# Rounding half of the output projection's inputs inside the attention, and issuing one half block there, in the two attention layers

## The reference, cut to what matters

```
# odd: 16 heads of 128, over the keys that a top-k picks
logits = einsum('bqhd,bqkd->bqhk', qb, kg) * (128 ** -0.5)
p = softmax(where(valid, logits, -inf));  o = einsum('bqhk,bqkd->bqhd', p, vg)
x = x + gate * ((o * silu(g)) @ odd_w_out)        # (512 x 2048) @ (2048 x 1024)
# fox: 16 heads of 64, causal, with a decay of the keys
x = x + (o * silu(gate)) @ fox_w_out              # (512 x 1024) @ (1024 x 1024)
```

## Time and profile before

| | us |
|---|---|
| median of 3 runs (lowest, highest) | 1831.99 (1830.11, 1836.62) |
| the profiled execution, its own time | 1826.95 |
| its span | 1825.2 |
| TensorE matmul busy | 1728.3 (95%) |
| VectorE busy | 1267.1 (69%) |
| GpSimd busy | 817.8 (45%) |
| ScalarE busy | 807.8 (44%) |

### The profile page before, as it was taken

One profiled execution on the slowest core, in us unless ns is written; L12 is line 12 of the kernel. 1 busy time (PEld: TensorE's weight loads), 2 busy tenths in 40 slices (PEclk: granted clock), 3 DMA queues, 4 the chain that ended last, 5 costly groups with the idle time before them and its releaser, 6 DMA issues.

```text
span 1825.2 us, 32731 instructions
## 1 busy us (share of the span) xinstructions
PE 1728.3 (95%) x13216; PEld 1282.1 (70%) x13216; DVE 1267.1 (69%) x2285; ACT 807.8 (44%) x1500; POOL 817.8 (45%) x721
## 2 busy tenths in 40 slices
PE   5999999999999979999999999899999999999987
PEld 5677777777777657767776666587677787777756
DVE  7599999999998676269986665634687617155553
ACT  3435345345343262365434443434577534344443
POOL 3534344344342245457871111255455555544433
PEclk9999999999999989999999999999999999999999
DMA  7212212212213124212221001022222232333312
GB/s 294 93 48 94 90 52 94 83 59 94 84 59 128 37 68 135 94 57 81 81 81 47 30 29 46 16 101 81 93 83 77 70 106 79 126 122 127 110 50 92
DMA packets 51878, 154.73 MB, mean 85 GB/s; under 512 B 5889, under 2 KB 12033, under 8 KB 51601
## 3 DMA queue, kind: packets, MB, share of 16 engines
q1 hardware_dynamic: 51728, 152.65, 24.9%
HBM read 150.50 MB, written 2.13 MB: 84 GB/s over the span
## 4 chain that ended last, share of the span: by engine, by line
PE 62%; DVE 19%; ACT 5%; issue 5%; POOL 5%; DMA 1%; DVEq 0%; SPq 0%; POOLq 0%; ACTq 0%
PE bank L504 14%; PE bank L508 13%; PE bank L505 13%; PE bank L1249 6%; PE bank L2244 3%; PE bank L2232 3%; PE bank L2266 2%; POOL w_lo L486 2%; DVE lru_xc L2686 2%; DVE best L2353 2%; DVE ya L1554 2%; DVE score L2356 2%; DVE raw L728 1%; PE bank L2899 1%; DMA raw<-even_in 1%
## 5 line engine op out<-in xcount | busy, mean ns | idle before, releaser
L486 POOL TENSOR_TENSOR w_lo<-raw,w_hi 128x512 fp32r<-128x512 f32 (+2 forms) x434 | 570.7, 1333 | 767.7 <-ACT w_hi L468 767.4
L504 PE MATMUL bank<-h_hi,w_hi 128*128 128x512 f32 x1368 | 585.4, 428 | 26.6 <-ACT h_hi L948 8.6
L508 PE MATMUL bank<-h_lo,w_hi 128*128 128x512 f32 x1368 | 545.2, 399 | 9.1 <-DVE h_lo L922 5.4
L505 PE MATMUL bank<-h_hi,w_lo 128*128 128x512 f32 x1368 | 541.8, 396 | 0.0
L468 ACT ACTIVATE w_hi<-raw 128x512 fp32r<-128x512 f32 (+2 forms) x434 | 241.9, 599 | 254.8 <-PE bank L508 179.9
L504 PEld LDWEIGHTS bank<-h_hi,w_hi 128*128 128x128 f32 x1368 | 261.8, 191 | 116.6 <-issue 48.3
L508 PEld LDWEIGHTS bank<-h_lo,w_hi 128*128 128x128 f32 x1368 | 260.7, 191 | 78.7 <-DVE h_lo L922 10.1
L505 PEld LDWEIGHTS bank<-h_hi,w_lo 128*128 128x128 f32 x1368 | 262.3, 192 | 57.1 <-issue 11.1
L1554 DVE SCALAR_TENSOR_TENSOR ya<-padded,vecs,ya 128x512 f32<-128x512 f32 x240 | 217.0, 904 | 3.3
L2301 ACT ACTIVATE probs<-probs,small 128x512 f32<-128x512 f32 x64 | 46.3, 724 | 108.9 <-DVE small L2284 108.5
L2968 DVE CUSTOM_DVE_ANT_0 fox_probs<-bank,fox_keybias 128x128 f32<-128x128 f32 (+3 forms) x64 | 28.8, 488 | 84.8 <-PE bank L2899 84.5
(11 more groups left out here) (398 smaller groups left out, 2796.6 us busy)
## 6 DMA issues: line engine op xcount, KB each, us to landing
raw<-even_in SPq DMA_DIRECT2D x57, 512.0 KB, 3.7
raw<-odd_in SPq DMA_DIRECT2D x39, 512.0 KB, 3.4
raw<-ada SPq DMA_DIRECT2D x32, 512.0 KB, 4.4
raw<-fox_in SPq DMA_DIRECT2D x25, 512.0 KB, 3.5
raw<-lru_in SPq DMA_DIRECT2D x24, 512.0 KB, 3.5
ada_first<-ada SPq DMA_DIRECT2D x16, 512.0 KB, 13.6
raw<-even_out SPq DMA_DIRECT2D x16, 512.0 KB, 3.5
raw<-odd_out SPq DMA_DIRECT2D x16, 512.0 KB, 3.4
```

The source lines that it names most:

```text
L486: e.tensor_tensor(k.w_lo[s % NSPLIT][:, at], k.raw[n % NRAW][:, at], k.w_hi[s % NSPLIT][:, at].bitcast(F32), ALU.subtract).then_inc(*did(" ...
L504: e.matmul(out, hi[:, w], x[i][0], start=start and i == 0, stop=False, skip_group_check=True)
L505: e.matmul(out, lo[:, w], x[i][0], start=False, stop=False, skip_group_check=True)
L508: m = e.matmul(out, hi[:, w], x[i][1], start=False, stop=stop and i == kt - 1, skip_group_check=True)
```

## The change: what it does, and the diff

1. In both layers the first half of the inputs (tiles 0 to 7 in odd, 0 to 3 in fox) is split inside the attention, after the last gate block is projected. ScalarE's `own_high` gets labels behind that block: 59.4 to 62.9 in odd (items 60 to 63 are the last), 30.7 to 31.6 in fox. GpSimd's `own_low` follows its last weight split of the stage.
2. Who makes the low parts: in odd all 8 of the first half are now GpSimd's (before, VectorE made 5 of them). In fox tiles 1 and 2 stay VectorE's, with labels 31.2 and 31.5, and 0 and 3 GpSimd's.
3. TensorE: half block (0,0) is issued between the attention's last transposes and products (labels 64.6 to 66.4 in odd, 32.3 to 33.1 in fox). Half block (1,0) stands behind the last product, as before.
4. The second half's splits wait for the last value product and for the last steps of VectorE, ScalarE and GpSimd in the attention (`attention_left`), and no longer for TensorE's last projection.

```
 def own_rest(s, i):
-    return ("made" if i % 3 else "pooled", "own_lo", s, i)
+    return ("pooled" if i % 3 == 0 or s == "odd" and i < AH // 2 else "made", "own_lo", s, i)
+def attention_left(k, stage, last):
+    return [("multiplied", *last)] + [("end", stage, engine) for engine in ("vector", "scalar", "gpsimd")]
...
+def out_block(k, e, need, did, s, name, pairs, cb, part, times):
...
+    return project(k, e, need, did, (name, cb, part), k.out_bank[cb], pairs[a:a + half],
+                   lambda i: [("activated", "own_hi", s, a + i), own_rest(s, a + i)], times, part == 0, part == 1)
...
+def og_time(i):
+    return gate_times(AH - 1)[-1] + 0.3 + 0.5 * i
...
 # odd_tensor
+    def out_blocks():
+        for cb in range(2):
+            at = AH * TT + 0.5 + 4 * cb
+            yield from out_block(k, e, need, did, "odd", "odd_out", k.odd_out[0], cb, 0, [at + (i + 0.5) / 4 for i in range(DT)])
     merge(in_tiles(AH * TT, (0, front), (LAG, back), (LAG + 1, at_head_end(finish))),
-          chain(*(block(("g", g), [("made", "gate", g)], gate_times(g)) for g in range(3, AH))))
+          chain(*(block(("g", g), [("made", "gate", g)], gate_times(g)) for g in range(3, AH)), out_blocks()))
...
 # odd_scalar
+    def early():
+        for i in range(AH // 2):
+            yield og_time(i)
+            own_high(e, need, did, "odd", i, k.odd_out[0], og_source(k), [("made", "og", i), ("projected", ("g", AH - 1))])
...
 # odd_gpsimd
     for g in range(3, AH):
         ahead(("g", g))
+    for i in range(AH // 2):
+        own_low(e, need, did, "odd", i, k.odd_out[0], og_source(k), [])
...
+def fox_y_time(i):
+    return fox_end("fox_g", DT - 1) + 0.1 + 0.3 * i
...
 # fox_tensor
+    def out_blocks():
+        for cb in range(2):
+            at = FOX_TILES + 0.2 + 3 * cb
...
 # fox_vector
+    def early():
+        for i in range(DT // 2):
+            if own_rest("fox", i)[0] == "made":
+                yield fox_y_time(i) + 0.2
+                own_low(e, need, did, "fox", i, k.fox_out[0], fox_y_source(k), [])
...
 # fox_scalar
+            yield fox_y_time(i)
+            own_high(e, need, did, "fox", i, k.fox_out[0], fox_y_source(k),
+                     [("made", "fox_y", i), ("projected", ("fox_g", DT - 1))])
...
 # fox_gpsimd
+    for i in range(DT // 2):
+        if own_rest("fox", i)[0] == "pooled":
+            own_low(e, need, did, "fox", i, k.fox_out[0], fox_y_source(k), [])
```

More of the change, by code:

```diff
@@ L247, in begin @@
         self.stat_until = ()
+        self.out_bank = {}
         if rehearsal:
@@ L954, in own_low, with out_tensor, out_scalar @@
     e.tensor_tensor(pairs[i][1], src(i), pairs[i][0].bitcast(F32), ALU.subtract).then_inc(*did(*own_rest(s, i)))
[L957 to L973, removed]
+def out_block(k, e, need, did, s, name, pairs, cb, part, times):
+    half = len(pairs) // 2
+    if part == 0:
+        k.out_bank[cb] = k.acc.take(("made", "x", s, cb))
+        k.bank[name, cb] = k.out_bank[cb][0]
+    a = part * half
+    return project(k, e, need, did, (name, cb, part), k.out_bank[cb], pairs[a:a + half],
+                   lambda i: [("activated", "own_hi", s, a + i), own_rest(s, a + i)], times, part == 0, part == 1)
+def out_tensor(k, e, need, did, s, name, pairs, sq, nxt, last=(), both=False, done=0):
+    times = out_times(len(pairs) // 2)
+    merge(*last, chain(*(out_block(k, e, need, did, s, name, pairs, cb, part, times[cb, part])
+                         for cb, part in out_order()[done:])))
     square_tensor(k, e, need, did, nxt, both, sq)
-def out_scalar(k, e, need, did, s, name, pairs, src, src_ready, sq, nxt, stage, last=(), beside=(), gain=None, early=0):
+def out_scalar(k, e, need, did, s, name, pairs, src, src_ready, sq, nxt, stage, last=(), beside=(), gain=None, early=0, free=None):
     n = len(pairs)
     def split(i):
-        own_high(e, need, did, s, i, pairs, src, [*src_ready(i), *k.ended(stage)])
+        own_high(e, need, did, s, i, pairs, src, [*src_ready(i), *(free or k.ended(stage))])
     def blocks():
@@ L1007, in out_vector @@
 def out_vector(k, e, need, did, s, name, pairs, src, src_ready, sq, nxt, stage, x_ready, gate=None, gate_ready=None,
-               last=(), beside=(), both=False, early=0):
+               last=(), beside=(), both=False, early=0, free=None):
     n = len(pairs)
     def split(i):
-        own_low(e, need, did, s, i, pairs, src, k.ended(stage))
+        own_low(e, need, did, s, i, pairs, src, free or k.ended(stage))
     def squares(i):
@@ L1045, in out_vector, with out_gpsimd @@
     merge(*last, *beside, blocks())
-def out_gpsimd(k, e, need, did, s, name, pairs, src, src_ready, stage, last=(), early=0):
+def out_gpsimd(k, e, need, did, s, name, pairs, src, src_ready, stage, last=(), early=0, free=None):
     n = len(pairs)
     def split(i):
-        own_low(e, need, did, s, i, pairs, src, k.ended(stage))
+        own_low(e, need, did, s, i, pairs, src, free or k.ended(stage))
     def blocks():
         yield 0.0
-        for i in range(early, n - 1, 3):
-            split(i)
+        for i in range(early, n - 1):
+            if own_rest(s, i)[0] == "pooled":
+                split(i)
         for b, (cb, part) in enumerate(out_order()):
@@ L2115, in gate_times, with og_source @@
     return [at + (i + 0.5) / 1.75 for i in range(DT)]
+def og_time(i):
+    return gate_times(AH - 1)[-1] + 0.3 + 0.5 * i
+def og_source(k):
+    return lambda i: k.Q[:, i, :]
 def turning(k, n):
@@ L2248, in odd_tensor @@
     turned = lambda i: [turn_done("odd", i)]
+    def out_blocks():
+        for cb in range(2):
+            at = AH * TT + 0.5 + 4 * cb
+            yield from out_block(k, e, need, did, "odd", "odd_out", k.odd_out[0], cb, 0, [at + (i + 0.5) / 4 for i in range(DT)])
     merge(in_tiles(AH * TT, (0, front), (LAG, back), (LAG + 1, at_head_end(finish))),
-          chain(*(block(("g", g), [("made", "gate", g)], gate_times(g)) for g in range(3, AH))))
+          chain(*(block(("g", g), [("made", "gate", g)], gate_times(g)) for g in range(3, AH)), out_blocks()))
     k.end("tensor", "odd")
-    out_tensor(k, e, need, did, "odd", "odd_out", *k.odd_out, "lru", both=True)
+    out_tensor(k, e, need, did, "odd", "odd_out", *k.odd_out, "lru", both=True, done=2)
     k.end("tensor", "odd_out")
@@ L2414, in odd_vector @@
                k.odd_out[1], "lru", "odd", lambda i: [("made", "x", "even", i)],
-               lambda i: k.mods[1][:, 2 * DT + i:2 * DT + i + 1], ("made", "mod", 1, 3 * DT - 1), both=True,
+               lambda i: k.mods[1][:, 2 * DT + i:2 * DT + i + 1], ("made", "mod", 1, 3 * DT - 1), both=True, early=AH // 2,
+               free=attention_left(k, "odd", ("attended", AH - 1)),
                beside=[lru_rates_vector(k, e, need, did), gain_squares_vector(k, e, need, did)])
@@ L2493, in back @@
             e.activation(dst, src, ACT.Copy).then_inc(*did("activated", "turned_odd", i))
-    merge(in_tiles(AH * TT, (0, middle), (LAG, back)), chain(*(gate_in(g, gate_times(g)[-1] + 0.2) for g in range(3, AH))))
+    def early():
+        for i in range(AH // 2):
+            yield og_time(i)
+            own_high(e, need, did, "odd", i, k.odd_out[0], og_source(k), [("made", "og", i), ("projected", ("g", AH - 1))])
+    merge(in_tiles(AH * TT, (0, middle), (LAG, back)), chain(*(gate_in(g, gate_times(g)[-1] + 0.2) for g in range(3, AH))), early())
     k.end("scalar", "odd")
     out_scalar(k, e, need, did, "odd", "odd_out", k.odd_out[0], lambda i: k.Q[:, i, :], lambda i: [("made", "og", i)],
-               k.odd_out[1], "lru", "odd", gain=lambda i: k.vec("final_g", i),
+               k.odd_out[1], "lru", "odd", gain=lambda i: k.vec("final_g", i), early=AH // 2,
+               free=attention_left(k, "odd", ("attended", AH - 1)),
                beside=[lru_rates_scalar(k, e, need, did)])
@@ L2536, in odd_gpsimd @@
         ahead(("g", g))
+    for i in range(AH // 2):
+        own_low(e, need, did, "odd", i, k.odd_out[0], og_source(k), [])
     k.end("gpsimd", "odd")
-    out_gpsimd(k, e, need, did, "odd", "odd_out", k.odd_out[0], lambda i: k.Q[:, i, :], lambda i: [("made", "og", i)], "odd")
+    out_gpsimd(k, e, need, did, "odd", "odd_out", k.odd_out[0], lambda i: k.Q[:, i, :], lambda i: [("made", "og", i)], "odd", early=AH // 2,
+               free=attention_left(k, "odd", ("attended", AH - 1)))
     k.end("gpsimd", "odd_out")
@@ L2917, in finish @@
         k.work.give(bank, ("made", "fox_y", p))
-    merge(projections(2, None), in_tiles(FOX_TILES, (0, front), (FOX_LAG + 1, at_pair_end(finish)), (FOX_LAG, back)))
+    def out_blocks():
+        for cb in range(2):
+            at = FOX_TILES + 0.2 + 3 * cb
+            yield from out_block(k, e, need, did, "fox", "fox_out", k.fox_out[0], cb, 0,
+                                 [at + (i + 0.5) / 4 for i in range(DT // 2)])
+    merge(chain(projections(2, None), out_blocks()),
+          in_tiles(FOX_TILES, (0, front), (FOX_LAG + 1, at_pair_end(finish)), (FOX_LAG, back)))
```

(8 more changed lines are left out.)

14 lines of the change are left out of this document (9 added, 5 removed).

## The result

| us | before | after |
|---|---|---|
| median, first comparison (6 runs each) | 1833.65 | 1824.26 (1819.45 to 1828.05) |
| ratio, 95% interval | | 0.9946 (0.9925 to 0.9966) |
| profiled execution; span | 1826.95; 1825.2 | 1823.81; 1822.1 |
| TensorE, VectorE busy | 1728.3, 1267.1 | 1729.5, 1260.3 |

The changed kernel is faster by 0.54% (0.34 to 0.75%). The forecast was a gain of 4.0 us, to 1828.0, with a range from 1822.5 to 1832.5. The median lies in the range, but the gain between the medians, 9.4 us, is more than twice the forecast, while the two profiled spans differ by 3.1 us only. Most of what follows is about that gap.

What follows compares the result with a forecast made beforehand. TensorE was taken as the bound (matmuls for 95% of the span), so time is won only where it idles or runs slowly. Odd 3.7 plus fox 1.7 less clock 1.4 gave 4.0 us gained, 1828.0 us, range 1822.5 to 1832.5.

Steps and rivals of the forecast that it cites:

- rival A: Whole kernel: full gain, no new low clock stretch or weights sooner than added up; 5.4 to 8 us gained; chance 0.33.
- same: Whole kernel: outcome within 0.3% (5.5 us), about what a measurement can tell from no change; chance 0.58.
- ScalarE's roundings push head 14's product to 1160.8: Odd's attention end: 4.2 us of new roundings delay the copy this product needs, and so its start, by only 1.2 us.
- Eight tiles ahead of the last product, none waiting for GpSimd; last product at 1171.5: Odd, TensorE: half block (0,0)'s 5.6 us stand ahead, low parts ready in time; last product starts 5.6 us later than 1165.94.
- A new wait for `w_lo` ahead of (0,1), start at 1181.9: Odd: weights come last, TensorE waits 1.2 us, and (0,1) starts at 1181.9 in place of 1185.63, 3.7 us gained.
- the list behind (0,1): Odd, TensorE: everything behind (0,1)'s start is the same instructions, busy 5.60 of 5.60 us, and moves as one.
- Fox, 1.7 us: Fox's tail: division 2.1 us late, last product 2.5, yet (0,1) 1.4 us earlier and tile 7 in time; 1.7 us gained.
- The contention rule set aside: Odd, VectorE divisions beside GpSimd subtractions: the skill's full-block rule would lose 5.4 us; one 0.53 us division was read against it.
- The clock, "one new low stretch in the two places", -1.4 us: Odd's and fox's tails: new TensorE idle times of 3.1 and 2.4 us bring one 1.2 GHz stretch, costing 1.4 us.
- "A shift in one stage carries over" to the median: Whole kernel: the profiled execution's 4.0 us gain passes to the median, which stands 5.0 us above it, giving 1828.0 us.

Runs made afterwards that it cites:

- e4: Changed kernel with half block (0,1)'s weight split moved ahead of the second half's roundings (ScalarE) and low parts (GpSimd), both layers: 1821.93 us, 0.9935 of the kernel before.
- e6: Changed kernel with VectorE again making five of odd's first eight low parts, as before the change: 1832.90 us, ratio 0.9997 to the kernel before.
- e3: Changed kernel with early roundings kept in both layers, but half block (0,0) put back behind the attention: 1829.09 us, ratio 0.9981 to the kernel before.
- c1: The kernel before, unchanged, timed against itself: 1831.71 us against 1834.56, ratio 0.9980.

## Why the prediction was right or wrong

The median fell inside the range, but partly by luck: the working holds 4.0 us of gain, and it was the width of the range that took in 9.4. The outcome is rival A's (1824 to 1826.5), whose condition, no new low stretch in the two tails, held in odd always and in fox in three of four profiles; its sum of 5.4 us is still not 9.4. Of the three outcomes, "same" had 0.58 and the one that came, faster by more than 0.3%, had 0.36.

- **ScalarE's roundings push head 14's product to 1160.8:** right, 1160.54; the copy ended 1.0 us later, forecast 1.2.
- **Eight tiles ahead of the last product, none waiting for GpSimd; last product at 1171.5:** right, 1170.92. GpSimd took 10.64 us for eight (1.33 each, forecast 1.35 to 1.70).
- **A new wait for `w_lo` ahead of (0,1), start at 1181.9:** right, 1.32 us, 1181.29; e4 shows its cause. From head 13's gating to (0,1) it is 4.4 us shorter, forecast 3.7. To (1,1) it is 3.75 shorter: the list behind (0,1) does not move as one, for (0,1) itself takes 6.2 us in place of 5.6, 0.28 of it the wait for a low part. The match with 3.7 at (1,1) is two misses that cancel.
- **Fox, 1.7 us:** right in size, 1.5 (32.7 to 31.15), by two misses that nearly cancel. The last item's division starts 2.1 us later against pair 6's gating (8.13 in place of 6.02), as forecast. But its two heads then took 1.71 us beside GpSimd in place of 0.86, and the last product starts 3.2 us later (11.23 in place of 8.01, at equal low time), forecast 2.5. From there to (0,1) it is 7.1 us, added up as 7.6, with a wait for `w_lo` of 1.7, not 2.4.
- **The contention rule set aside:** this step was wrong, and the row that it leaned on was misread. That division, of 0.53 us, had met only the last 0.24 us of GpSimd's subtraction. These are GpSimd's single subtractions beside it, beside the division at 1158.40 after, and beside that at 1168.27 in e6:

```profile
1153.71 1.27 POOL L486 TENSOR_TENSOR w_lo<-raw,w_hi 128x512 fp32r<-128x512 f32 x1 [15.97 <-ACT w_hi L468]
...
1157.84 1.26 POOL L961 TENSOR_TENSOR h_lo<-q,h_hi 128x512 fp32r<-128x512 f32 x1
...
1168.09 1.26 POOL L961 TENSOR_TENSOR h_lo<-q,h_hi 128x512 fp32r<-128x512 f32 x1 [4.49 <-ACT h_hi L955]
```

  They end at 1154.98, 1159.10 and 1169.35; the divisions end at 1155.27, 1159.38 and 1169.64, each 0.28 to 0.29 us behind. In the 14 traces, all 221 of odd's 128x512 divisions that start while a GpSimd subtraction runs end 0.28 to 0.29 us behind it; those that meet none take 0.49. They took 0.50 to 1.47 us. So the division is held until the running subtraction ends, and its price goes by when it starts: 0.01 us near the end of a subtraction, up to 0.98 near its start. This agrees with the full block of the Trainium skill (SBUF — State Buffer, "Who interferes with whom"). It cost little in odd, where the last four divisions took 0.52, 0.98, 0.51 and 0.85 us, 0.9 us more in all than four of 0.49, and VectorE then waited 2.85 us for the product. In fox it is the 0.85 us of the point above.
- **The clock, "one new low stretch in the two places", -1.4 us:** this step failed. Odd's tail lost its low stretch and got none, in four of four; fox's has one in one of four. Behind the same 2.50 us of idle time the clock fell in e3 and not in the changed kernel. Instead the clock is low in two norms behind the tails, where TensorE's work is the same; the stages that hold them are 0.9 us longer each:

```profile
1263.23 3.78 PE L862 MATMUL bank<-ident,rms 128*128 128x128 f32 x16 [0.89 <-DVE rms L888]
...
1811.89 2.08 PE L862 MATMUL bank<-ident,rms 128*128 128x128 f32 x8 [0.56 <-DVE rms L871]
```

  In three of the four profiles of before these took 2.05 and 1.16 us. In the fourth, c1, they are as slow as now, and a third norm between them took 2.07 us in place of 1.16:

```profile
1265.26 3.79 PE L861 MATMUL bank<-ident,rms 128*128 128x128 f32 x16 [0.90 <-DVE rms L887]
...
1820.37 2.07 PE L861 MATMUL bank<-ident,rms 128*128 128x128 f32 x8 [0.57 <-DVE rms L870]
```

  So the kernel before loses more in some executions (c1: 700.9 us in the last four stages, where the first profile of before has 693.4), and the changed kernel had the slow norms in four of four. I priced the clock by one new low stretch in the two tails alone. I gave no price to the norms behind them, nor to the chance that the clock falls further in the old passage.
- **"A shift in one stage carries over" to the median:** it does for the stages, not for the comparison. Of the first 9.4 us, 5.3 stand in the tails, -1.8 in the norms, and about 2 in the average over executions like c1. The 4 us that are left are not placed; a kernel showed 2.9 us against itself. That split is worked out, not measured apart; what lengthens the common stretch from 1128.2 to 1137.5 us beside its low time (17 to 34 us) stays open.

## What to carry to other kernels

Round or load what the next stage needs while the last tiles of this one still wait, but look at what each engine has queued between: the new bound was a weight split queued behind the second half's roundings (seven in odd), and putting it first gave 4 us more in the two tails. Give such early work to the engine that the chain of waits does not pass (GpSimd here, not VectorE). Before a row is taken to show that two engines don't disturb each other, look at how long they overlapped in it. Measure by the same instructions in several profiles: at equal low time the tails repeat to 0.1 us here, where medians of one kernel differ by 2.9.

## What the runs showed of the hardware that I had not expected

A VectorE division (128x512) that starts while a GpSimd subtraction runs ends 0.28 to 0.29 us behind it, in 221 of 221 cases. In 177 of them it started so near the subtraction's end that it took under 0.6 us in place of 0.49, so a row picked by chance shows next to no loss.

The clock's falls repeat from execution to execution at the same instructions (odd's tail 3.4 us of low time in all four profiles of before; the norm behind it slow in all four of after). With the early work moved by a few us they stand in stages whose instructions are unchanged, though the kernel before also shows them there in one profile of four. And over 6 to 29 timed runs of a kernel the time goes with the mean granted clock by 1.1 to 1.8 us for each 0.001, near the 1.8 us (1825 x 0.001, an estimate) that TensorE would lose if it were busy all the time.
